# Linear attention's sample part: six state slots, one product of 40 rows to spread the values, and steps moved between the value copies

## The reference

```python
log_a = log_sigmoid(low @ w_gate2 + b_gate2) / 16          # per key column
S_new = exp(log_a)[:, None] * S_old[b, h] + k[:, None] * v[None, :]
o     = (q * 128 ** -0.5) @ S_new
o     = o * rsqrt(mean(o * o) + 1e-5) * norm_g * silu(r)    # then @ w_out
```

## Time and profile before

| | |
|---|---|
| median of 3 runs | 1884.14 us (1883.71 to 1886.66) |
| profiled execution | 1878.84 us, of it span 1876.8 us |
| PE busy | 1674.6 us, 89% of the span |
| DVE, ACT, POOL busy | 633.0, 549.1, 722.6 us |
| stretch of this phase | about 1253 to 1410 us |

### The profile page before, as it was taken

How to read it: one execution, slowest core, us unless ns; L and a number is a source line. 1 busy time by engine, 2 the same in 40 slices (tenths; PEclk the granted TensorE clock), 3 DMA queues, 4 the chain that set the end, 5 groups by cost and what they waited for, 6 DMA issues and landing times. The chain is left out here.

```text
span 1876.8 us, 37967 instructions
## 1 busy us (share of the span) xinstructions
PE 1674.6 (89%) x15074; PEld 1520.0 (81%) x15074; DVE 633.0 (34%) x1282; ACT 549.1 (29%) x1064; POOL 722.6 (39%) x510
## 2 busy tenths in 40 slices
PE   4699798869878869899999998998889899999996
PEld 4599677646656649899999997987659899999996
DVE  1211110434454546611111128326465711111127
ACT  1222000135544433432222213216432432222311
POOL 3453232323335436554434325503026564434320
PEclk8899799679999989899999998998979999999998
DMA  6633887035535524143223223222404143223201
GB/s 224 197 89 110 244 261 243 12 115 181 158 114 157 160 73 142 53 133 97 85 85 102 81 67 90 82 67 68 146 12 138 54 135 91 87 84 105 85 15 46
DMA packets 297172, 210.54 MB, mean 112 GB/s; under 512 B 34286, under 2 KB 290467, under 8 KB 296483
## 3 DMA queue, kind: packets, MB, share of 16 engines
q1 hardware_dynamic: 278490, 166.27, 30.2%
q10 hardware_dynamic: 10696, 21.78, 3.6%
q0 software_dynamic: 7808, 20.05, 3.5%
HBM read 197.97 MB, written 18.42 MB: 115 GB/s over the span
## 5 line engine op out<-in xcount | busy, mean ns | idle before, releaser
L1593 PE MATMUL ps<-x_high,w_high_t 128*128 128x256 f32 (+1 forms) x1488 | 427.3, 287 | 12.5 <-POOL w_low_t L1516 7.6
L1516 POOL TENSOR_TENSOR w_low_t<-w_raw,w_high_t 128x1024 fp32r<-128x1024 f32 (+1 forms) x130 | 307.7, 2376 | 326.8 <-ACT w_high_t L1621 326.8
L1594 PE MATMUL ps<-x_low,w_high_t 128*128 128x256 f32 (+1 forms) x1488 | 423.4, 285 | 0.0
L1595 PE MATMUL ps<-x_high,w_low_t 128*128 128x256 f32 (+1 forms) x1488 | 422.7, 284 | 0.0
L1593 PEld LDWEIGHTS ps<-x_high,w_high_t 128*128 128x128 f32 x1488 | 283.8, 191 | 16.2 <-POOL x_low L1526 7.9
L1594 PEld LDWEIGHTS ps<-x_low,w_high_t 128*128 128x128 f32 x1488 | 283.6, 191 | 0.3
L1595 PEld LDWEIGHTS ps<-x_high,w_low_t 128*128 128x128 f32 x1488 | 282.9, 190 | 0.0
L1621 ACT CAST w_high_t<-w_raw 128x1024 fp32r<-128x1024 f32 (+1 forms) x130 | 132.1, 1025 | 147.8 <-PE ps L1595 123.5
L1705 DVE TENSOR_TENSOR h_t<-silu_t,ps 128x256 f32<-128x256 f32 (+1 forms) x88 | 37.4, 425 | 359.4 <-PE ps L1595 354.9
L1593 PE MATMUL ps<-hid_high,w_high_t 128*128 128x264 f32 (+1 forms) x542 | 154.4, 285 | 0.0
L1594 PE MATMUL ps<-hid_low,w_high_t 128*128 128x264 f32 (+1 forms) x542 | 153.6, 283 | 0.0
(11 more groups left out here) (338 smaller groups left out, 3263.6 us busy)
## 6 DMA issues: line engine op xcount, KB each, us to landing
w_raw<-in_ffn_w_gu SPq DMA_DIRECT2D x88, 512.0 KB, 3.8
pages<-in_cache_slc SPq DMA_DIRECT2D x192, 128.0 KB
rows<-in_cache_cmp SPq DMA_DIRECT2D x123, 128.0 KB, 4.0
w_raw<-in_ffn_w_down SPq DMA_DIRECT2D x32, 448.0 KB, 3.7
w_raw<-in_gla_w_in SPq DMA_DIRECT2D x24, 512.0 KB, 3.6
rows<-in_cache_cmp ACTq DMA_DIRECT2D x70, 128.0 KB, 5.1
pages<-in_cache_slc POOLq DMA_DIRECT2D x64, 128.0 KB, 2.8
w_raw<-in_ffn_w_down SPq DMA_DIRECT2D x16, 512.0 KB, 4.0
```

Of the source, the lines that this page charges most:

```text
L1516: nc.gpsimd.tensor_tensor(low(u)[:, 0:k], raw[:, u % RAW, 0:k], high(u)[:, 0:k].bitcast(F32), ALU.subtract).then_inc(low_done, 1)
L1593: nc.tensor.matmul(psum(i), high(u)[:, k, :], a[0][:, at, c], start=(k == 0), stop=False)
L1594: nc.tensor.matmul(psum(i), high(u)[:, k, :], a[1][:, at, c], start=False, stop=False)
L1595: ins = nc.tensor.matmul(psum(i), low(u)[:, k, :], a[0][:, at, c], start=False, stop=(k == t.kc - 1))
```

## The change

The samples' values now lie in one tile `vs` of 40 partitions: rounded values in partitions 0 to 7, the rest in 32 to 39, zeros between (POOL clears them at the phase's start). `pick` has 40 rows, and one product replaces two. The step "vs" makes both and stands with "as" (the samples' exponents) right after the scan; "decay" stands before pass 7; "qd" and "scale_q" stand after the first sample's spreads. There are six slots, three of them loaded at the start as before, and three after the last value transpose. The four key transposes stand before the last sample's spreads, pass 13 before the last output; pass 14 alone stands between "kv" 0 and 1.

```diff
-    SS, LOW0, LM = 4, 3072, 32
+    SS, EARLY, LOW0, LM = 6, 3, 3072, 32
...
-              ("logsig", 0), ("scan", 0), ("pass", 5), ("vt", 4), ("vt", 5), ("pass", 6), ("vt", 6), ("vt", 7), ("pass", 7),
-              ("vt", 8), ("vt", 9), ("decay", 0), ("qd", 0), ("scale_q", 0)]
+              ("logsig", 0), ("scan", 0), ("as", 0), ("vs", 0), ("pass", 5), ("vt", 4), ("vt", 5), ("pass", 6), ("vt", 6),
+              ("vt", 7), ("decay", 0), ("pass", 7), ("vt", 8), ("vt", 9)]
     for b in range(NB):
+        if b == NB - 1:
+            ORDER += [("kt", t) for t in range(TILES)]
         ORDER += [("s", 2 * b), ("s", 2 * b + 1)]
+        if b == 0:
+            ORDER += [("qd", 0), ("scale_q", 0)]
         ORDER += [[("scale_k", 0)], [("scale_end", 0)], []][min(b, 2)]
         if b in (0, 1, 3, 4, 6):
             ORDER.append(("pass", 8 + (0, 1, 3, 4, 6).index(b)))
         if b:
             ORDER.append(("so", b - 1))
-    ORDER += [("kt", 0), ("kt", 1), ("so", NB - 1), ("kt", 2), ("kt", 3), ("sfin", 0), ("att", 0), ("att", 1)]
+    ORDER += [("pass", 13), ("so", NB - 1), ("sfin", 0), ("att", 0), ("att", 1)]
...
-            ORDER += [("pass", 13), ("pass", 14)]
+            ORDER.append(("pass", 14))
...
+        HI, LO = slice(0, NB), slice(32, 32 + NB)
+        vs = nc.alloc_sbuf_tensor_at("g_vs", [32 + NB, D_MODEL], F32R, offset=att_at)
+        pick = nc.alloc_sbuf_tensor_at("g_pick", [32 + NB, NB, P], F32R, offset=ep_at + 4 * 2 * GH * SEQ)
...
+        early = sb("s_state", [P, EARLY, GH, 256])
+        late = nc.alloc_sbuf_tensor_at("g_s_late", [P, SS - EARLY, GH, 256], F32, offset=T["o_at"] + 4096)
+        sst = [early[:, i] for i in range(EARLY)] + [late[:, i] for i in range(SS - EARLY)]
...
-            state_in(SS - 1)
+            for b in range(EARLY, SS):
+                state_in(b)
...
+            nc.gpsimd.memset(vs[0:LO.start].bitcast(F32), 0.0).then_inc(vs_zero, 1)
...
-                    pool.wait_ge(so_done, NB)
+                    pool.wait_ge(spread, 2 * NB)
                     nc.gpsimd.memset(att[:], 0.0).then_inc(att_zero, 1)
...
-                nc.tensor.matmul(ps[:, SPREAD + w % 3, :], pick[:, b, :], vs_high[:, half], start=True, stop=False)
-                nc.tensor.matmul(ps[:, SPREAD + w % 3, :], pick[:, b, :], vs_low[:, half], start=False, stop=True)\
+                nc.tensor.matmul(ps[:, SPREAD + w % 3, :], pick[:, b, :], vs[:, half], start=True, stop=True)\
                     .then_inc(spread, 1)
...
-                elif kind == "qd":
+                elif kind == "vs":
                     for c in range(2):
                         taken(act, ("vt", c))
-                    nc.scalar.copy(vs_high[:], v[0:NB, NT - 1, :]).then_inc(vs_done, 1)
+                    act.wait_ge(vs_zero, 1)
+                    nc.scalar.copy(vs[HI], v[0:NB, NT - 1, :]).then_inc(vs_done, 1)
...
+                elif kind == "vs":
+                    nc.vector.tensor_tensor(pick[:], cst["ident"][0:LO.stop, HI].unsqueeze(2).to_broadcast([LO.stop, NB, P]),
+                                            cst["ident"][0:LO.stop, LO].unsqueeze(2).to_broadcast([LO.stop, NB, P]),
+                                            ALU.add).then_inc(pick_ready, 1)
                     dve.wait_ge(vs_done, 1)
-                    nc.vector.tensor_tensor(vs_low[:], v[0:NB, NT - 1, :], vs_high[:].bitcast(F32), ALU.subtract)\
+                    nc.vector.tensor_tensor(vs[LO], v[0:NB, NT - 1, :], vs[HI].bitcast(F32), ALU.subtract)\
                         .then_inc(vs_split, 1)
```

More of the change, by code:

```diff
@@ L1850, in phase_gla @@
         att = sb("att", [P, 2, GH, P])
-        vs_high = nc.alloc_sbuf_tensor_at("g_vs_high", [NB, D_MODEL], F32R, offset=att_at)
-        vs_low = nc.alloc_sbuf_tensor_at("g_vs_low", [NB, D_MODEL], F32R, offset=T["o_at"] + 4096)
-        pick = nc.alloc_sbuf_tensor_at("g_pick", [NB, NB, P], F32R, offset=T["o_at"] + 8192)
+        HI, LO = slice(0, NB), slice(32, 32 + NB)
+        vs = nc.alloc_sbuf_tensor_at("g_vs", [32 + NB, D_MODEL], F32R, offset=att_at)
+        pick = nc.alloc_sbuf_tensor_at("g_pick", [32 + NB, NB, P], F32R, offset=ep_at + 4 * 2 * GH * SEQ)
         mask, reset = sb("mask", [P, P], I32), sb("reset", [P, SEQ])
         sst_at = nc.sbuf_base
-        state3 = sb("s_state", [P, SS - 1, GH, 256])
-        sst = [state3[:, i] for i in range(SS - 1)]
-        sst.append(nc.alloc_sbuf_tensor_at("g_s_state3", [P, GH, 256], F32, offset=T["o_at"] + 12288)[:])
+        early = sb("s_state", [P, EARLY, GH, 256])
+        late = nc.alloc_sbuf_tensor_at("g_s_late", [P, SS - EARLY, GH, 256], F32, offset=T["o_at"] + 4096)
+        sst = [early[:, i] for i in range(EARLY)] + [late[:, i] for i in range(SS - EARLY)]
         on = nc.alloc_sbuf_tensor_at("g_on", [P, 2, GH, 256], F32, offset=sst_at)
@@ L1875, in phase_gla @@
         kv_done, st_done, att_zero = sem("kv"), sem("st"), sem("att_zero")
-        pick_ready, vs_done, vs_split, qd_zero, qd_ready = (sem(n) for n in ("pick", "vs_done", "vs_split", "qd_zero", "qd"))
+        pick_ready, vs_done, vs_split, qd_zero, qd_ready, vs_zero = (sem(n) for n in ("pick", "vs_done", "vs_split", "qd_zero", "qd", "vs_zero"))
         squared, std, rstd, silu, xh_done, xl_done, s_squared, s_std, s_rstd, sxh_done = (
@@ L1934, in _ @@
             sp.dma_start(reset[:], io["gla_reset_tab"]).then_inc(tab, 16)
-            for b in range(SS - 1):
+            for b in range(EARLY):
                 state_in(b)
@@ L2195, in _ @@
                     take_v(nc.scalar.copy, n)
-                elif kind == "decay":
+                elif kind == "as":
                     act.wait_ge(logsig, 1)
                     nc.scalar.activation(as_[:], z[:, :, SEQ:NTOK], ACT.Exp, scale=1.0 / GLA_TAU).then_inc(as_done, 1)
+                elif kind == "decay":
                     act.wait_ge(lb_ready, 1)
@@ L2352, in _ @@
                     dve.wait_ge(qd_zero, 1)
-                    nc.vector.tensor_copy(pick[:], cst["ident"][0:NB, 0:NB].unsqueeze(2).to_broadcast([NB, NB, P]))\
-                        .then_inc(pick_ready, 1)
                     diag = qd[:].rearrange("p h b x -> p h (b x)")[:, :, 0:NB * 33 - 32:33]
                     nc.vector.tensor_scalar(diag, T["qk"][:, 0:GH, SEQ:NTOK], GSCALE, None, ALU.mult).then_inc(qd_ready, 1)
+                elif kind == "vs":
+                    nc.vector.tensor_tensor(pick[:], cst["ident"][0:LO.stop, HI].unsqueeze(2).to_broadcast([LO.stop, NB, P]),
+                                            cst["ident"][0:LO.stop, LO].unsqueeze(2).to_broadcast([LO.stop, NB, P]),
+                                            ALU.add).then_inc(pick_ready, 1)
                     dve.wait_ge(vs_done, 1)
-                    nc.vector.tensor_tensor(vs_low[:], v[0:NB, NT - 1, :], vs_high[:].bitcast(F32), ALU.subtract)\
+                    nc.vector.tensor_tensor(vs[LO], v[0:NB, NT - 1, :], vs[HI].bitcast(F32), ALU.subtract)\
                         .then_inc(vs_split, 1)
```

## The result

| | before | changed |
|---|---|---|
| median, first comparison | 1883.99 us (4 runs) | 1870.09 us (4 runs), ratio 0.9923 (95%: 0.9905 to 0.9940) |
| median, second comparison | 1881.90 us (11 runs) | 1871.34 us (6 runs), ratio 0.9939 (0.9923 to 0.9954) |
| profiled span | 1876.8, again 1878.7 us | 1867.4, again 1869.8 us |
| the phase in those traces | 156.9, 158.5 us | 146.7, 146.7 us |

What lies outside it varied by 10 us over the fourteen traces (1716.9 to 1726.7) with no relation to the edits, so the experiments are read inside the phase. The change is worth 10.2 to 11.8 us there, and the medians say 13.9 and 10.6.

What follows compares the result with a forecast made beforehand. PE, 89% busy, was held by two holes and their low clock; first output product 15.4 us earlier, less 1.7 for clock, gives 13.7 off the median: 1870.4 us, range 1866.0 to 1877.5.

Steps and rivals of the forecast that it cites:

- First hole: PE's 7.12 us idleness between last value transpose and first spread: removed, first spread at 1288.6, ACT's 2.5 us covered.
- Product: One 40-row spread product replaces two: 0.65 us a pair, 5.2 us for eight instead of 9.0.
- Waits for DVE: PE waits for state updates before sixth spread, second output, eighth and fourteenth spread: 5.25 us in all.
- the 4.48 feared: POOL's low-part subtraction for a weight unit, slowed from 2.34 to 4.48 us beside DVE's two-input work.
- Clock: PE's clock falls in the new sparse stretch, 1296.7 to 1302.5, costing 1.7 us.
- 4.23 us hole: PE's old wait before the eighth sample output; nearest row for the clock: 0.72 in 6 us, 1.7 lost.
- signs of being wrong: Wait for `pick` or low part over 1 us, spread step 0.4, state 6/7 wait, 0.5 clock over 6 us.
- Rival (b): DVE's queue binds: POOL's subtraction takes 4.48, state 1 1.6 us later, clock loss 4.0; 9.8 off, 1874.3; 18%.
- Second hole: PE's wait before the eighth sample output, from late state transfers: six slots close it with 9 us to spare.
- `kv0`: First kv step after the sample part: 38 to 41 us after the last value transpose, before 50.4.
- `kv0` to the first output product: `kv1` 4.1 us after `kv0` instead of 7.04, then 4.81 unchanged to the prompt's first output product.

Runs made afterwards that it cites:

- four_slots: The changed kernel with four slots instead of six: 1870.67 us (6 runs), phase 146.6 us.
- scales_spread: The changed kernel with `scale_k` moved behind the third sample's spreads and `scale_end` behind the fifth's: 1866.59 us (6 runs), phase 141.9.
- between_two_products: passes_between with every spread product issued twice: 1871.78 us (1 run), phase 143.2 us.
- passes_between: The changed kernel with pass 10 between spreads five and six, 11 between seven and eight, 12 behind the twelfth: 1864.37 us (6 runs).

## Why the prediction was right, and where not

The forecast was 1870.4 (13.7 us off), the time 1870.09. The mechanism was right in the main, the amount by luck: up to the first output product the profiled pair gave 10.2 us, where the forecast's sum stood at 13.7. Step by step, from the last value transpose's end (1288.58 there, 1289.39 in the new trace):

- First hole: the first spread followed at once; ACT's three instructions cost pass 5's copy nothing that PE saw; `pick` over 40 partitions took 1.19, as taken.
- Product: a pair of 40 rows takes 0.66 us from its start to the pass's (1289.32 to 1289.98), as forecast (0.65). Doubling cost 3.8 us in the old order, where PE is full, as the forecast's 9.0 - 5.2 = 3.8, but only 1.4 in the changed order, where waits take up the rest.
- Waits for DVE: forecast 1.95, 0.55, 2.1 and 0.65, measured 1.78, 0.28, 2.84 and 0.57, 5.5 for 5.25, at the same four instructions. The third is longer because `scale_end` took 3.44 instead of 2.28 beside POOL's subtraction. I had named the pair but charged it to POOL alone (3.19 us for its subtraction, of the 4.48 feared).
- Clock: the term that was too small. I took 1.7 us, from the 4.23 us hole, and one stretch of 3 to 4 us. Measured: 10.5 us at 0.53, pass 10 alone 2.4 longer, the eighth spread 0.30 and the third output 0.26, about 3 us in all. One of my signs of being wrong came true with it, a clock of 0.5 in more than 6 us after the eighth spread (6.43). Rival (b), DVE's queue as the bound with a clock loss of 4.0, is close in amount, 9.8 off against 10.2; but its cause, state 1 held up 1.6 us by POOL's subtraction, is not: the delay sat in `scale_end`, before state 2.
- Second hole: closed, but not, as I wrote, by the slots. four_slots shows that the new order alone gives the transfers their time; in the old order the slots carry most of the gain. The slots and the product give 8.9 to 9.3 of the 10.2 to 10.6 us without the new order, which adds 1.3.
- `kv0` 43.1 us after the last transpose (forecast 38 to 41, a miss), `kv0` to the first output product 8.95 (forecast 8.9).

From the transpose to `kv0` the sum with its clock term is 39.65 and the trace 43.13. Of the 3.5 between them, 1.3 have come by when the eighth spread goes, 1.3 are clock beyond the 1.7, and 0.9 are passes of 3.04 to 3.11 us where I took 2.97, the key transposes (2.4 for 2.2) and other small gaps. The time agreed nevertheless because the first four runs of before lay 2.1 us above the 1881.9 of 11 later ones, and the first four of the changed kernel 1.3 below the 1871.3 of six later ones.

## What to carry to other kernels

When a hole in front of a chain is removed, work out what the chain's next supplier can deliver; here DVE's 8 us of bulk work ahead of small urgent updates took the whole gain back, and moving PE's independent passes into those waits gave more than the reorder itself (8 us against 1.3). Price a sparse stretch by the clock of what comes after it, not by its idle time. Undo the parts both ways: slots worth 5 us in one order were worth nothing in the other. And end the measured stretch where the edits end: here the untouched rest of the phase alone moved by 1.2 us, as much as the new order was worth.

## What the runs showed of the hardware that I had not expected

- The clock fell without a long hole: in scales_spread no wait of PE between the first spread and 1303 was over 0.95 us, and it still ran at 0.72 in the 6 us from 1300; in between_two_products a wait of 0.45 us stood before 4.90 us at 0.65, and in passes_between one of 1.15 us before none. After the changed kernel's sparse stretch it took 10.5 us to come back, although PE was busy without a gap for the last 6.4 of them.
- Of DVE's and POOL's two-input operations, the one that started second was slowed, by about the overlap, and the first was not. POOL's subtraction at 1289.95 beside DVE's difference (1288.59 to 1290.88, its usual 2.29) took 3.19 instead of 2.34; DVE's `scale_end` at 1300.29 beside POOL's subtraction (1299.20 to 1301.58, its usual 2.38) took 3.44. Alone, in scales_spread, it took its usual time. The fourteen traces agree: POOL's subtraction took 3.18 to 3.22 us in the seven where it starts inside DVE's difference and 2.34 to 2.35 in the seven others, `scale_end` 3.42 to 3.48 in the six where it starts inside POOL's subtraction and 2.28 in the eight others. DVE's state updates, with one input from PSUM, were not slowed and did not slow (1.65 at 1298.72, across the start of POOL's 2.38 at 1299.20).

```profile
1308.67 2.28 DVE L2348 TENSOR_TENSOR g_a<-g_a,gla_qk 128x2048 f32<-128x2048 f32 x1
```
